# First heads of each attention turned earlier, the exponential table fetched earlier, stacked keys turned twice

## The reference

```
def joint_dense_attention(q, k, v, kc, vc):
    ...
    sc = jnp.einsum('bqkgd,bnkd->bkgqn', qi, kk, preferred_element_type=jnp.float32) * (d ** -0.5)
    p = jax.nn.softmax(sc, axis=-1)
    return jnp.einsum('bkgqn,bnkd->bqkgd', p.astype(vv.dtype), vv)
...
cum_logf = jnp.cumsum(jax.nn.log_sigmoid((f_logit + b_forget).astype(jnp.float32)), axis=1)
```

## Time and profile before

| | |
|---|---|
| three runs | 1711.34, 1712.95, 1714.96 us |
| median | 1712.95 us |
| profiled execution | 1713.2 us, its span 1711.4 us |
| mean granted clock of PE | 0.963 of full speed |
| busy | PE 94%, DVE 53%, ACT 38%, POOL 33% of the span |

### The profile page before, as it was taken

How to read it: one execution, slowest core, us unless ns; L and a number is a source line. 1 busy time by engine, 2 the same in 40 slices (tenths; PEclk the granted TensorE clock), 3 DMA queues, 4 the chain that set the end, 5 groups by cost and what they waited for, 6 DMA issues and landing times.

```text
span 1711.4 us, 24961 instructions
## 1 busy us (share of the span) xinstructions
PE 1606.0 (94%) x9200; PEld 1349.0 (79%) x9200; DVE 902.9 (53%) x2097; ACT 652.5 (38%) x1331; POOL 566.1 (33%) x333
## 2 busy tenths in 40 slices
PE   4999889898999979998999999989999999999998
PEld 1788878797998858887888789956578778887787
DVE  2656737665665244923743797036521379916422
ACT  3322354344554223334542433344323343336332
POOL 1222231860001333446505344310423534431134
PEclk8999999798999989999999999969999999999999
DMA  8321213231013212331003232200112222220222
GB/s 329 84 73 46 63 51 89 73 88 50 26 38 112 62 31 81 91 95 61 2 13 92 84 99 84 89 1 1 50 50 87 99 82 99 99 74 1 84 89 86
DMA packets 93158, 124.41 MB, mean 73 GB/s; under 512 B 10288, under 2 KB 52208, under 8 KB 92016
## 3 DMA queue, kind: packets, MB, share of 16 engines
q1 hardware_dynamic: 93040, 122.82, 22.7%
HBM read 120.70 MB, written 2.10 MB: 72 GB/s over the span
## 4 chain that ended last, share of the span: by engine, by line
PE 85%; DVE 7%; ACT 3%; issue 2%; DMA 1%; POOL 1%; SPq 0%; DVEq 0%; ACTq 0%; POOLq 0%
PE psum L842 18%; PE psum L844 18%; PE psum L843 18%; PE psum L1039 9%; PE psum L1027 5%; PE psum L1004 3%; PE psum L957 3%; PE psum L812 3%; PE psum L997 1%; DMA mod_w<-mod_w_in 1%; PE psum L1000 1%; PE psum L901 1%; PE psum L998 1%; PE psum L1002 1%; PE psum L1001 1%
## 5 line engine op out<-in xcount | busy, mean ns | idle before, releaser
L1758 POOL TENSOR_TENSOR wlo<-wraw,whi 128x1024 fp32r<-128x1024 f32 (+4 forms) x172 | 398.5, 2318 | 970.9 <-ACT whi L1090 970.8
L1090 ACT ACTIVATE whi<-wraw 128x1024 fp32r<-128x1024 f32 (+4 forms) x172 | 174.7, 1019 | 483.4 <-PE psum L844 483.4
L842 PE MATMUL psum<-whi,h2h 128*128 128x512 f32 (+2 forms) x800 | 309.6, 387 | 6.9 <-ACT buf L1139 5.8
L844 PE MATMUL psum<-whi,h2l 128*128 128x512 f32 (+2 forms) x800 | 305.7, 382 | 0.0
L843 PE MATMUL psum<-wlo,h2h 128*128 128x512 f32 (+2 forms) x800 | 305.3, 382 | 0.0
L842 PE MATMUL psum<-whi,hTh 128*128 128x512 f32 (+2 forms) x512 | 197.1, 385 | 9.5 <-DVE hTl L1463 7.3
L843 PE MATMUL psum<-wlo,hTh 128*128 128x512 f32 (+2 forms) x512 | 192.1, 375 | 0.0
L844 PE MATMUL psum<-whi,hTl 128*128 128x512 f32 (+2 forms) x512 | 191.7, 374 | 0.0
L1238 ACT ACTIVATE pr<-psum,nmax 128x768 f32<-128x768 f32 (+2 forms) x208 | 137.9, 663 | 131.8 <-DVE nmax L1559 83.1
L842 PEld LDWEIGHTS psum<-whi,h2h 128*128 128x128 f32 x800 | 150.7, 188 | 32.9 <-issue 7.9
L844 PEld LDWEIGHTS psum<-whi,h2l 128*128 128x128 f32 x800 | 150.5, 188 | 27.0
(11 more groups left out here) (263 smaller groups left out, 2626.4 us busy)
## 6 DMA issues: line engine op xcount, KB each, us to landing
wraw<-mod_w_in SPq DMA_DIRECT2D x32, 512.0 KB, 3.6
wraw<-w_in_odd_in SPq DMA_DIRECT2D x32, 512.0 KB, 3.4
wraw<-cd_w_in_in SPq DMA_DIRECT2D x24, 512.0 KB, 3.6
wraw<-w_in_even_in SPq DMA_DIRECT2D x20, 512.0 KB, 3.8
mod_w<-mod_w_in SPq DMA_DIRECT2D x8, 1024.0 KB, 17.6
wraw<-ab_w_in_in SPq DMA_DIRECT2D x16, 512.0 KB, 3.6
wraw<-w_ple_gate_in SPq DMA_DIRECT2D x16, 512.0 KB, 3.8
wraw<-ab_w_out_in SPq DMA_DIRECT2D x8, 512.0 KB, 3.6
```

Source lines behind the costliest of these rows:

```text
L842: eng.matmul(dst, a[0], ww[0], start=first, stop=False)
L844: mm = eng.matmul(dst, a[1], ww[0], start=False, stop=last_)
L1090: eng.activation(whi[:, s, :, 0:w], wraw[:, u["id"] % RAW, :, 0:w], ACT.Copy).then_inc(*to("split_hi", u["id"]))
L1758: eng.tensor_tensor(wlo[:, s, :, 0:w], wraw[:, u["id"] % RAW, :, 0:w], f32(whi[:, s, :, 0:w]), ALU.subtract)\
```

## The change

The functions of the new kernel have lines of their own: in it L993/L995 are the turns (L957 before), L1242 ACT's copy of a turned head (L1207/L1213), L1133 `split_hi`, L1182 the evacuation, L1279 the exp, L1070 and L1082 the turns of the probabilities and the products with the values, L869 to L871 the weight matmuls.

1. `BEFORE`: first heads of gqa, win, diff and odd are turned by PE ahead of the matmuls of a late chunk of the stage before: keys ahead of chunk 2 of up, 5 of in2, 7 of in3, 6 of in4, queries ahead of the next chunk. The wait for all norms stands at the first of these turns. `BEHIND`: first heads of mla are turned at units 47 and 48 of gqa's loop, those of fox at 31 and 32 of diff's, in banks 0 to 3.
2. Stacked keys: each tile is turned into partitions 0 to 63 and again, by an ordinary matmul with ident, into 64 to 127. One ACT copy and one DVE subtract of 128 partitions take the place of two each. Six matmuls more for each of four key groups.
3. `exp_table()`: an Exp of the sink (esink, read by nobody) at unit 0 of chunk 2 of up, after in2, after in3 and after in4. The Exp and Ln of the log gates move into chunk 7 of in3.
4. `LEADS`: ACT's splits for the first two units of out1, out2, out3 and out4 move into mla (units 40, 43) and win, fox, odd (units 2, 3). POOL does the convolution and the norms of diff's result ahead of its first low parts of out2 and out3.

```
+        BEFORE = {"gqa": {("up", 2): (0, 2), ("up", 3): (2, 4)}, "win": {("in2", 5): (0, 2), ("in2", 6): (2, 3)},
+                  "diff": {("in3", 7): (0, 1), ("in3", 8): (1, 2)}, "odd": {("in4", 6): (0, 1), ("in4", 7): (1, 2)}}
+        LEADS = {("mla", 40): ("out1", 0), ("mla", 43): ("out1", 1), ("win", 2): ("out2", 0), ("win", 3): ("out2", 1),
+                 ("fox", 2): ("out3", 0), ("fox", 3): ("out3", 1), ("odd", 2): ("out4", 0), ("odd", 3): ("out4", 1)}
+        BEHIND = {"gqa": "mla", "diff": "fox"}
...
@@ tensor: products
+                    for what in first_heads((name, ci)):
+                        prep(*what)
                     product(c, operand_ready, lambda i, ci=ci: groups_at(ci, i))
...
+            def prep(name, p_):
+                key, _, rows, tiles, _, d = p_
+                if p_[0] == prep_times(name)[-1][0][0]:
+                    for w_ in ready_of[name]:
+                        eng.wait_ge(*at(*w_))
+                b, m_ = prep_bank(name, p_), turned_rows(name, p_)
+                bank_free(b)
+                for n_, t in enumerate(tiles):
+                    mm = eng.transpose(psum[0:min(m_, DK[name]), b, n_ * P:(n_ + 1) * P], rows(t), ident[:, :])
+                    if m_ > DK[name]:
+                        mm = eng.matmul(psum[DK[name]:m_, b, n_ * P:(n_ + 1) * P], rows(t), ident[:, :], start=True, stop=True)
...
@@ scalar: attention
+                    for what in next_heads(name, j):
+                        prep(*what)
+                    if (name, j) in LEADS:
+                        lead, n_ = LEADS[name, j]
+                        split_hi(ahead_of(lead)[n_])
...
@@ scalar: program
-            ahead("out2")
+            exp_table()
             attention("win")
...
+                if where == ("in3", 7, 2):
+                    eng.wait_ge(*at("vector", ("fabs",)))
+                    eng.activation(fexp[:, :, :], fexp[:, :, :], ACT.Exp, scale=-1.0).then_inc(*to("f_exp", 0))
+                    eng.wait_ge(*at("f_exp", 0))
+                    eng.activation(fexp[:, :, :], fexp[:, :, :], ACT.Ln, bias=1.0).then_inc(*to("f_exp", 1))
...
@@ gpsimd: program
+            conv()
             ahead("out2")
-            conv()
             products("out2", "in3")
+            sub_norms()
             ahead("out3")
-            sub_norms()
```

More of the change, by code:

```diff
@@ L944, in running_sums, with attention @@
                 reader[7] = ("vector", ("fcum",))
-            def attention(name, ready):
+            ready_of = {
+                "gqa": [("vector", ("normed", n_, t)) for n_ in ("gk", "gq") for t in ALL],
+                "mla": [("gpsimd", ("normed", n_, t)) for n_ in ("mq", "mk") for t in ALL] + [evac_of("up3", t) for t in ALL],
+                "win": [("vector", ("normed", "wk", t)) for t in ALL] + [("vector", ("normed", "wq", t)) for t in XT],
+                "diff": [("vector", ("normed", n_, t)) for n_ in ("qa", "ka") for t in XT],
+                "fox": [("vector", ("normed", n_, t)) for n_ in ("qb", "kb") for t in XT] + [("vector", ("fcum",))],
+                "odd": [("vector", ("normed", n_, t)) for n_ in ("q0", "q1", "k0", "k1") for t in XT]}
+            values_of = {"diff": ("in32",), "fox": ("in35", "in36"), "odd": ("in44", "in45")}
+            def prep(name, p_):
[9 more added lines that the diff above has]
+                        mm = eng.matmul(psum[DK[name]:m_, b, n_ * P:(n_ + 1) * P], rows(t), ident[:, :], start=True, stop=True)
+                mm.then_inc(*to("heads_turned", (name, key)))
+                reader[b] = copied(name, p_)
+            def attention(name):
                 qT, kT, pr, prT = temps(name)
@@ L1073, in _ @@
             products("in4")
-            attention("odd", [("vector", ("normed", n_, t)) for n_ in ("q0", "q1", "k0", "k1") for t in XT]
-                      + [evac_of(n_, t) for n_ in ("in44", "in45") for t in XT])
+            attention("odd")
             products("out4")
@@ L1187, in products, with prep @@
                 evacuations(flat[-1][3]["chunk"])
+            def prep(name, p_):
+                key, _, _, tiles, dst, d = p_
+                if name not in ROUNDED and p_[0] in [q_[0] for q_ in prep_times(name)[-1]]:
+                    return
+                eng.wait_ge(*at("heads_turned", (name, key)))
+                out_ = parts_of(name, p_)[0][0] if name in ROUNDED else dst
+                eng.activation(out_, psum[0:out_.shape[0], prep_bank(name, p_), 0:len(tiles) * P], ACT.Copy)\
+                   .then_inc(*to("heads_copied", (name, key)))
             def square_rows(tag, tiles, halves=(0, 1)):
@@ L1285, in _, with exp_table @@
             ahead("in1")
+            def exp_table():
+                loads[0] += 1
+                eng.activation(esink[:, :], sink[:, 0:4], ACT.Exp).then_inc(*to("exp_table", loads[0]))
+            loads = [0]
             def tables(where):
+                if where == ("up", 2, 0):
+                    exp_table()
                 if where != ("in1", 1, 2):
```

119 lines of the change are left out of this document (56 added, 63 removed).

## The result

Nineteen runs of each kernel gave a median of 1703.67 us (1694.59 to 1712.26) for the changed one and 1713.88 us (1710.0 to 1719.94) for the one before; the ratio is 0.994, with an interval of 0.9923 to 0.9958. So the change gains 10.2 us where 22.3 were forecast. Run twice more as an experiment (e5, e13), the same kernel gave ratios of 0.9957 and 0.9936.

The account below looks back on a forecast made before the run. PE, busy 1606.0 of 1711.4 us, was taken as the bound, with idle time and half clock to be saved. Gains less the stall and splits summed to 22.3 us, from 1713.2 to 1690.9 us; range 1678 to 1705.

Parts of the forecast that it names:

- the price of the stacked turns: Four key groups in gqa and win: six extra ordinary matmuls cost PE 1.3 us per group, 5.3 in all.
- gqa's unit 23: Second stacked key group in gqa: copies go, the turn grows, less half clock behind it; 2.5 us gained.
- gqa start: Start of gqa: scores follow the last product at once, less idle and half clock; 3.7 us gained.
- mla start: Start of mla: turns move into waits of gqa's last units, less idle and half clock; 5.0 us gained.
- win start: Start of win: most of the 6.62 us idle and the half clock after it go; 6.0 us gained.
- win unit 23: Second stacked key group in win: casts go from the 3.20 us wait, less half clock; 2.0 us gained.
- fox start: Start of fox: turns behind diff's last units remove the wait for fk and small waits; 2.5 us gained.
- odd start: Start of odd: the table load and the wait for DVE's qT go; 2.3 us gained.
- Stall ahead of chunk 6: In in4: PE stands 6.4 us for k1's norm before odd's key turn, plus 2.3 us lost at half clock.
- diff start: Start of diff: moving gates and splits removes idle and half of the half-clock loss; 6.0 us gained.
- The splits: Eight ACT splits of 1.0 us moved inside the attentions, mostly into slack; net cost 1.0 us.
- the clock falls as before: Rival for the whole kernel: no clock gain, only 8.5 us saved, 1704.7 us; chance 0.20.

Follow-up runs that it names:

- e5: The changed kernel itself run again, unedited, in the second group of experiments; 1707.9 us, ratio 0.9957 to the kernel before.
- e13: The changed kernel itself run a third time, unedited, in the fourth group of experiments; 1702.9 us, ratio 0.9936 to the kernel before.
- e16: Changed kernel with the first heads of mla and fox turned at the start of their attention as before; 1713.3 us, ratio 0.9988.
- e1: Changed kernel with odd's first key head turned ahead of chunk 7 of in4 instead of chunk 6; 1695.1 us, ratio 0.987.
- e8: Changed kernel without the four early fetches of the exponential table, log gates staying in chunk 7; 1704.6 us, ratio 0.9934.
- e3: Changed kernel with each stacked key group's turns batched, transposes first, then ordinary matmuls, instead of alternating; 1691.5 us, ratio 0.9857.
- e7: Changed kernel with ACT's out1 to out4 splits back ahead of win, diff and odd and behind mla, after the early table; 1713.7 us, ratio 1.0003.
- e6: Changed kernel with odd's key head turned ahead of chunk 7 and both turns of stacked key tiles as ordinary matmuls; 1683.6 us, ratio 0.9821.
- e14: Changed kernel with odd's key head turned ahead of chunk 7 and stacked keys made as in the kernel before; 1682.6 us, ratio 0.9821.
- e15: Changed kernel with odd's late key turn, stacked turns as ordinary matmuls, and 12 filling transposes at gqa's unit 23; 1678.0 us, ratio 0.9796.

## Why the prediction was off

The forecast was right in direction, and the range (1678 to 1705) holds the time, near its slow end; but it said 22.3 us, and 10.2 were measured. The steps that failed are the price of the stacked turns (5.3 us forecast, 11.6 measured) and gqa's unit 23 (+2.5 forecast, −9.1 in the first profile). By the forecast's own steps, measured by matching instructions of the profile of 1707 us with those of the kernel before (in brackets the forecast, gains positive, turns charged where they stand, so that each of the four places with stacked keys bears its own 2.9 us where the forecast had charged 1.3):

- *gqa start* 2.5 (3.7), *mla start* 6.3 (5.0), *win start* 4.3 (6.0), *win unit 23* 1.4 (2.0), *fox start* 2.6 (2.5), *odd start* 3.7 (2.3): right in mechanism and near in size. mla and fox are confirmed by e16, which loses 4.9 and 2.2 us at these two places (5.0 and 2.5 forecast).
- *Stall ahead of chunk 6* −9.2 (−8.7): the idle time is exact, 6.40 us against 6.4, and the half clock came behind it. e1 takes it away. That it came out so exact was in part luck: in the 13 profiles that have this wait it is 6.4 us in eight, 5.3 in four and 8.0 in one (e8), within the 2 us that the forecast allowed for POOL's splits.
- *diff start* 10.6 (6.0): mis-sized for the good, one stretch of 20 us at half clock follows instead of two of 17. *diff, running sums* −1.9 (2.0): the stretch that is left lies around it.
- **Failed: the cost of the stacked turns.** I priced six ordinary matmuls from L919, which stands among its own kind, at 1.3 us a group. Alternating with transposes they add 2.9 us, 11.6 in all instead of 5.3: 1.06 us of the 1.6 too little per group are the alternation (e3), about 0.5 the matmuls in this setting.
- **Failed: gqa's unit 23**, −9.1 (2.5) in this profile. The group is long (2.9 of the 9.1 us), a wait of 1.41 us stays in it, and 17.1 and 13.7 us at half clock follow where the kernel before had two stretches of 10.2. That the long turns bring the low clock oftener is what the windows above suggest; it isn't shown. In e5's profile the same term comes to +2.3, as forecast, and the execution took 1691.6 us, near the predicted 1690.9. I had chosen one value for something that differs between executions of one binary; the median execution doesn't have the good luck.
- *The splits* (−1.0): wrong in what the gain was put down to, though not in the sum. Taking them back costs 7.9 us (e7), with PE waiting for the first exp at win and for ACT's copy of the next key at diff and odd. The forecast had charged them as work in ACT's slack and had put the starts' gains down to heads and table. The table brought nothing that the runs can tell (e8).
- A stretch of 6.8 us at half clock in in3, 2.9 us, that no step of mine had.

The measured terms, the splits left aside, come to +8.3; less the 2.0 us of the first 40 us that is 6.3, and the two spans differ by 6.0. The profile took 3.5 us longer than the median run.

Of the signs named beforehand, the scores without idle at win's start, the turn of probabilities about 4 us later, the wait ahead of chunk 6 and the full clock at most starts came true. Two did not: PE's busy time rose, and at win, diff and odd a table load still stands between the first scores and the first exp.

The rival *the clock falls as before* gave 1704.7, next to the measured median, but that is luck for the most part: win, odd and the starts of gqa and mla kept the full clock in the first profile; the clock fell elsewhere, and the dear turns did the rest. The mean clock over the change's 19 runs goes from 0.964 to 0.975, nearly in the order of their times (1712.3 to 1694.6 us). Span times clock is 1647 to 1654 us in all of them, and 1711.4 × 0.963 = 1648 for the kernel before. The product counts work and full-clock waits together, and by it the change shortened nothing: what it took away in waits it put back in turns and in the stall. In e6, e14 and e15, without these two costs, the product is 1635 to 1641 us. Over the last seven stages of the table, length less PE's busy time went from 71.1 to 61.0 us, so 16.5 us of waits went and the stall of 6.4 came; the extra matmuls cost 11.6. By this account what is left of the gain, some 10 us, comes from running less of it at half clock.

## What to carry to other kernels

Price an added instruction next to the kind of neighbours that it will have, since changing between transposes and matmuls cost 1.06 us per six pairs here, and two matmuls that write different halves of the partitions can run side by side. When work is moved ahead in an in-order queue, move its wait too: a wait for all inputs placed one chunk too early gave back 9 us here, and one line undid it. An early fetch helps only if the instructions queued ahead of it let it come early. Where the clock at a place differs between executions of one binary, profile several executions before giving a stretch one value, and look at time times clock to see whether work or clock has changed.

## What the hardware did that I had not expected

- A transpose and an ordinary f32 matmul into the two halves of a bank take 0.59 us as an alternating pair; six of each, batched by kind, take 2.47 us; twelve ordinary matmuls, two halves side by side, 1.46 us.
- One binary, one chip, 18 to 21 us between executions (e13: 1691.48 to 1712.89), nearly all of it in stretches at 1.2 GHz whose place changes, gqa's unit 23 and win's above all: span times clock spreads over only 6 us. The kernel before spread over 10 us.
- What decides whether such a stretch comes stays open. The same wait of 1.41 us preceded it at gqa's unit 23 in the first profile, in e5's and in e13's, at clocks of 0.71, 0.93 and 0.76.
